# Token-major projections in 512-column matmuls over two k-halves, and rotations placed first in their panel

## What is computed

```python
# first block, layer 0 (even mixer): 512 + 256 tokens
px = hx @ w_in_even; pc = hc @ w_in_even          # each (tokens, 8 * 512)
qa, ka, va, ga, bb, cb, ub, gb = split(px, 8)      # qa, ka are rotated (axial_rope); va is the V of attention
out_b = short_conv(bb, cb, ub, conv_w) * silu(gb)
# first block, layer 1 (odd mixer)
qn, kn, vn, gn, ud, gd = split(hx @ w_in_odd, 6)   # vn is the V of neighbourhood attention
# second block, layer 1: chunked spatial gating
z = gelu(h @ sgu_w_in)                             # (512, 2 * 3072)
u, v = split(z, 2)
v = layer_norm(v, ln_g, ln_b)                      # over 3072 features of a token
sv = einsum("gts,bcsgd->bctgd", tril(w_s), v_chunks) + b_s
out = (u * sv) @ w_out
```

## Time and profile before

| | |
|---|---|
| median of 3 runs | 2531.35 us (2530.65 to 2531.72) |
| the profiled execution | 2530.41 us, of which the span of instructions is 2528.7 us |
| TensorE matmul (PE) | 2335.9 us busy, 92% |
| VectorE (DVE) | 1411.4 us busy, 56% |
| ScalarE (ACT) | 589.1 us busy, 23% |
| GpSimd (POOL) | 88.3 us busy, 3% |
| mean granted TensorE clock | 0.935 of full speed |
| DMA | 196.03 MB, mean 78 GB/s |

### The profile page before, as it was taken

The page is one execution under the profiler, slowest core; times in us unless marked ns, Lnnn a source line. Parts: engine busy times, 40 slices in busy tenths (PEclk is TensorE's granted clock), DMA queues, the critical chain, the costliest instruction groups (busy, mean ns, idle before and its releaser), DMA issues.

```text
span 2528.7 us, 28943 instructions
## 1 busy us (share of the span) xinstructions
PE 2335.9 (92%) x12276; PEld 1911.6 (76%) x12276; DVE 1411.4 (56%) x1673; ACT 589.1 (23%) x1138; POOL 88.3 (3%) x57
## 2 busy tenths in 40 slices
PE   6999898999899978886799999999999999999997
PEld 5787786678879744675478888889988787888886
DVE  2332346774561177565857776354388735777633
ACT  2111015661320256125621111011110001111100
POOL 0000000000000122022100000000000000000000
PEclk9899998669799989997899999999999999999998
DMA  8022130001122101120012222322222122222222
GB/s 337 18 100 100 67 117 34 18 1 51 34 84 67 68 24 57 62 72 1 34 67 85 99 100 79 103 85 84 101 82 83 65 91 97 84 100 100 79 92 79
DMA packets 30704, 196.03 MB, mean 78 GB/s; under 512 B 3440, under 2 KB 3696, under 8 KB 12528
## 3 DMA queue, kind: packets, MB, share of 16 engines
q1 hardware_dynamic: 29136, 188.03, 21.1%
q10 hardware_dynamic: 1440, 6.16, 0.7%
HBM read 192.08 MB, written 2.10 MB: 77 GB/s over the span
## 4 chain that ended last, share of the span: by engine, by line
PE 84%; DVE 11%; ACT 2%; issue 1%; POOL 1%; DMA 1%; SPq 0%; DVEq 0%; ACTq 0%; POOLq 0%
PE ps L329 20%; PE ps L330 20%; PE ps L331 20%; PE ps L385 3%; PE ps L386 3%; PE ps L387 3%; PE ps L482 2%; PE ps L556 2%; PE ps L438 2%; PE ps L767 1%; PE ps L744 1%; PE ps L587 1%; PE ps L422 1%; PE ps L920 1%; PE ps L463 1%
## 5 line engine op out<-in xcount | busy, mean ns | idle before, releaser
L1414 DVE CAST whi<-raw 128x2048 fp32r<-128x2048 f32 (+2 forms) x162 | 183.8, 1135 | 482.2 <-DMA raw<-in_ffn_out 117.4
L329 PE MATMUL ps<-h2hi,whi 128*128 128x512 f32 x1040 | 409.4, 394 | 18.3 <-DVE h2lo L1511 12.1
L330 PE MATMUL ps<-h2lo,whi 128*128 128x512 f32 x1040 | 407.0, 391 | 0.0
L331 PE MATMUL ps<-h2hi,wlo 128*128 128x512 f32 x1040 | 406.7, 391 | 0.0
L1415 DVE TENSOR_TENSOR wlo<-raw,whi 128x2048 fp32r<-128x2048 f32 (+2 forms) x162 | 341.5, 2108 | 5.6
L329 PE MATMUL ps<-h1hi,whi 128*128 128x512 f32 (+1 forms) x768 | 278.0, 362 | 16.1 <-DVE h1lo L1456 8.0
L330 PE MATMUL ps<-h1lo,whi 128*128 128x512 f32 (+1 forms) x768 | 272.7, 355 | 0.0
L331 PE MATMUL ps<-h1hi,wlo 128*128 128x512 f32 (+1 forms) x768 | 270.6, 352 | 0.0
L329 PEld LDWEIGHTS ps<-h2hi,whi 128*128 128x128 f32 x1040 | 196.7, 189 | 61.2 <-issue 13.8
L331 PEld LDWEIGHTS ps<-h2hi,wlo 128*128 128x128 f32 x1040 | 196.7, 189 | 40.9
L330 PEld LDWEIGHTS ps<-h2lo,whi 128*128 128x128 f32 x1040 | 196.9, 189 | 40.5
(11 more groups left out here) (247 smaller groups left out, 3583.4 us busy)
## 6 DMA issues: line engine op xcount, KB each, us to landing
raw<-in_ffn_in SPq DMA_DIRECT2D x44, 1024.0 KB, 4.8
raw<-in_ffn_out SPq DMA_DIRECT2D x32, 704.0 KB, 4.1
raw<-in_even SPq DMA_DIRECT2D x16, 1024.0 KB, 6.9
mod_w<-in_mod SPq DMA_DIRECT2D x6, 2048.0 KB, 25.6
mraw<-in_mod SPq DMA_DIRECT2D x12, 1024.0 KB, 4.9
raw<-in_odd SPq DMA_DIRECT2D x12, 1024.0 KB, 4.9
raw<-in_sgu_v SPq DMA_DIRECT2D x12, 1024.0 KB, 4.8
raw<-in_sgu_u SPq DMA_DIRECT2D x12, 1024.0 KB, 4.8
```

The lines of the kernel that those rows point to most:

```text
L329: pe.matmul(o, r(lhi), r(rhi), start=first, stop=False, **kw)
L330: pe.matmul(o, r(lhi), r(rlo), start=False, stop=False, **kw)
L331: return pe.matmul(o, r(llo), r(rhi), start=False, stop=last, **kw)
L1414: step(dve.tensor_copy(whi[:, slot, 0:width].bitcast(F32R), raw[:, slot, 0:width]))
```

## The change

The three token-major projections are stored in DRAM in another order (`_wide_panels`): a pair of panels now holds 512 output features, the first panel the blocks kt 0 to 3 of them and the second the blocks 4 to 7. Each panel has the size that it had. A token tile's matmuls are 512 columns wide, fill a bank of their own, and accumulate over both panels; the banks of a pair stay taken from its first panel to the end of its second. In the second panel each tile is finished by itself and told by a new semaphore `wide_done` (the last by `panel_done`), and ScalarE evicts tile by tile, 512 columns at a time.

In the even projections the banks are handed over in other steps: panel 4 begins after `e_free` 3, panel 6 after `e_free` 5 (which ScalarE now tells after the third tile of the pair), and panels 7, 8 and 9 wait for `e_free` 6, 7 and 8. In the spatial gating the first pair fills banks 0 to 3 and the second banks 4 to 7: panel 2's first two tiles run before the spread, the third after it, and the fourth after the copy of the spread (`rx_copied`), since it takes bank 7.

VectorE's `rope(3)` stands ahead of the loop over j, and inside it `rope(4 + 2j)` and `rope(5 + 2j)` take the places of `rope(3 + 2j)` and `rope(4 + 2j)`, for j < 2: each of the rotations 4 to 7 stands one place earlier than it did.

```diff
...
+        EV_BANK, OV_BANK = (0, 1, 4, 2, 3, 5), (0, 1, 2, 3, 4, 5)
...
-            def paced_token_pair(n, hi, lo, parts_made):
-
-                pe.wait_ge(split_done, n + 2)
-                for kt in range(KT):
-                    pe.wait_ge(parts_made, kt + 1)
-                    for i in range(2):
-                        for t in range(4):
-                            last = token_part(n + i, 2 * i, t, kt, hi, lo, kt == 0 and t % 2 == 0,
-                                              kt == KT - 1, skip_group_check=True)
-                        if kt == KT - 1:
-                            last.then_inc(panel_done, 1)
+            def wide_part(n, bank, t, kt, hi, lo):
+
+                o = ps[:, bank, :]
+                lhi, llo = r(hi[:, kt, t * P:(t + 1) * P]), r(lo[:, kt, t * P:(t + 1) * P])
+                rhi, rlo = r(w(n, 0, kt % 4, width=512, cols=512)), r(w(n, 1, kt % 4, width=512, cols=512))
+                pe.matmul(o, lhi, rhi, start=kt == 0, stop=False)
+                pe.matmul(o, lhi, rlo, start=False, stop=False)
+                return pe.matmul(o, llo, rhi, start=False, stop=kt == KT - 1)
+
+            def wide_tile(n, half, bank, t, hi, lo):
+
+                for kt in range(4 * half, 4 * half + 4):
+                    last = wide_part(n, bank, t, kt, hi, lo)
+                return last
+
+            def wide_second_half(n, banks, hi, lo):
+
+                pe.wait_ge(split_done, n + 1)
+                for t, bank in enumerate(banks):
+                    last = wide_tile(n, 1, bank, t, hi, lo)
+                    if t < len(banks) - 1:
+                        last.then_inc(wide_done, 1)
+                last.then_inc(panel_done, 1)
...
-                if e in (4, 6, 8):
-                    pe.wait_ge(e_free, e)
+                if e in (6, 7, 8, 9):
+                    pe.wait_ge(e_free, e - 1)
                 elif e >= 10:
                     pe.wait_ge((zed, b_free)[s], (e - 8) // 2)
                 elif e in (2, 3):
                     pe.wait_ge(e_free, e - 1)
-                if e in (4, 5):
-                    token_panel(e, 3 * s, 6, h1hi, h1lo)
+                if e == 4:
+                    pe.wait_ge(split_done, e + 1)
+                    for t in range(6):
+                        if t in (0, 3):
+                            pe.wait_ge(e_free, 3 + t // 3)
+                        last = wide_tile(e, 0, EV_BANK[t], t, h1hi, h1lo)
+                    last.then_inc(panel_done, 1)
+                elif e == 5:
+                    wide_second_half(e, EV_BANK, h1hi, h1lo)
                 elif e == 0:
...
-            pe.wait_ge(o_free, 7)
-            token_panel(p0 + 8, 0, 6, h1hi, h1lo)
-            pe.wait_ge(o_free, 8)
-            token_panel(p0 + 9, 3, 6, h1hi, h1lo)
+            pe.wait_ge(split_done, p0 + 9)
+            for t in range(6):
+                if t in (0, 3):
+                    pe.wait_ge(o_free, 7 + t // 3)
+                last = wide_tile(p0 + 8, 0, OV_BANK[t], t, h1hi, h1lo)
+            last.then_inc(panel_done, 1)
+            wide_second_half(p0 + 9, OV_BANK, h1hi, h1lo)
...
-            paced_token_pair(p0, h2hi, h2lo, n_ok["mixpre1"])
+            for kt in range(KT):
+                if kt % 4 == 0:
+                    pe.wait_ge(split_done, p0 + kt // 4 + 1)
+                pe.wait_ge(n_ok["mixpre1"], kt + 1)
+                for t in range(4):
+                    last = wide_part(p0 + kt // 4, t, t, kt, h2hi, h2lo)
+                if kt % 4 == 3:
+                    last.then_inc(panel_done, 1)
             sums_added("mixpre1")
-            token_panel(p0 + 2, 4, 4, h2hi, h2lo)
+            pe.wait_ge(split_done, p0 + 3)
+            for t in range(2):
+                wide_tile(p0 + 2, 0, 4 + t, t, h2hi, h2lo)
             spread("mixpre1", range(4))
-            for n in range(3, 12):
-                pe.wait_ge(sg["v"], 4 * (n - 2))
-                token_panel(p0 + n, 2 * (n % 3), 4, h2hi, h2lo)
+            wide_tile(p0 + 2, 0, 6, 2, h2hi, h2lo)
+            pe.wait_ge(rx_copied, 3)
+            wide_tile(p0 + 2, 0, 7, 3, h2hi, h2lo).then_inc(panel_done, 1)
+            wide_second_half(p0 + 3, range(4, 8), h2hi, h2lo)
+            for g in range(2, 6):
+                base = 4 * (g % 2)
+                pe.wait_ge(split_done, p0 + 2 * g + 1)
+                for t in range(4):
+                    pe.wait_ge(sg["v"], 4 * (g - 2) + t + 1)
+                    last = wide_tile(p0 + 2 * g, 0, base + t, t, h2hi, h2lo)
+                last.then_inc(panel_done, 1)
+                wide_second_half(p0 + 2 * g + 1, range(base, base + 4), h2hi, h2lo)

             pe.wait_ge(sg["ws"], 1)
-            pe.wait_ge(sg["v"], 44)
+            pe.wait_ge(sg["v"], 20)
...
-                    pe.wait_ge(rx_copied, 3)
-                    pe.wait_ge(sg["v"], 48)
+                    pe.wait_ge(sg["v"], 24)
...
-                if e // 2 == 2:
-                    act.wait_ge(panel_done, e + 1)
-                    last = copy(ev[:, :, s * 256:(s + 1) * 256].rearrange("p (b t) n -> p b t n", t=2),
-                                ps[:, 3 * s:3 * s + 3, :].rearrange("p b (t n) -> p b t n", t=2))
+                if e == 4:
+                    continue
+                if e == 5:
+                    for t in range(6):
+                        if t < 5:
+                            act.wait_ge(wide_done, t + 1)
+                        else:
+                            act.wait_ge(panel_done, e + 1)
+                        last = copy(ev[:, t, :], ps[:, EV_BANK[t], :])
+                        if t == 2:
+                            tell(last, e_free, 5)
+                        elif t < 5:
+                            step(last)
...
+                if b < 4 or b == 5:
+                    act.wait_ge(panel_done, FIRST["odd"] + k + 1)
                 if b == 4:
-                    at = (0, 3)[s]
-                    last = copy(ov[:, :, s * 256:(s + 1) * 256].rearrange("p (b t) n -> p b t n", t=2),
-                                ps[:, at:at + 3, :].rearrange("p b (t n) -> p b t n", t=2))
+                    for t in range(3 * s, 3 * s + 3):
+                        if t < 5:
+                            act.wait_ge(wide_done, 6 + t)
+                        else:
+                            act.wait_ge(panel_done, FIRST["odd"] + 10)
+                        last = copy(ov[:, t, :], ps[:, OV_BANK[t], :])
+                        if t % 3 < 2:
+                            step(last)
...
-            for n in range(12):
-                b = 2 * (n % 3)
-                act.wait_ge(panel_done, FIRST["sgu_v"] + n + 1)
+            for g in range(6):
                 for t in range(4):
-                    copy(vtok[:, 2 * n:2 * n + 2, t, :],
-                         ps[:, b + t // 2, t % 2 * 256:t % 2 * 256 + 256].rearrange("p (d n) -> p d n", d=2),
+                    if g and t < 3:
+                        act.wait_ge(wide_done, 10 + 3 * (g - 1) + t + 1)
+                    else:
+                        act.wait_ge(panel_done, FIRST["sgu_v"] + 2 * g + 2)
+                    copy(vtok[:, 4 * g:4 * g + 4, t, :],
+                         ps[:, 4 * (g % 2) + t, :].rearrange("p (d n) -> p d n", d=4),
...
+            rope(3)
             for j in range(4):
-                if j < 3:
-                    rope(3 + 2 * j)
+                if j < 2:
+                    rope(4 + 2 * j)
                 split_at(9 + 2 * j)
                 dve.wait_ge(cb_in, j + 1)
                 step(dve.tensor_tensor(zpad[:, 514:770], eob[:, j, TX:TA], ps[:, 4, TC:2 * TC], ALU.mult))
                 tell(dve.tensor_tensor(zpad[:, 1:513], eob[:, j, 0:TX], ps[:, 1, :], ALU.mult), zed, j + 1)
                 if j < 2:
-                    rope(4 + 2 * j)
+                    rope(5 + 2 * j)
...
             def v_stats(i):
-                dve.wait_ge(sg["v"], 8 * (i + 1))
+                dve.wait_ge(sg["v"], 4 * (i + 1))
...
+def _wide_panels(w):
+
+    k, n = w.shape
+    return w.reshape(2, k // 2 // P, P, n // 512, 512).transpose(3, 0, 2, 1, 4).reshape(n // 256, P, -1)
...
```

More of the change, by code:

```diff
@@ L205, in build_kernel @@
         mod_rows, mod_cols = sem("mod_rows"), sem("mod_cols")
+        wide_done = sem("wide_tile_done")
         cond_ready = sem("cond_ready")
@@ L1166, in odd_out @@
                 b, s = k // 2, k % 2
-                act.wait_ge(panel_done, FIRST["odd"] + k + 1)
+                if b < 4 or b == 5:
+                    act.wait_ge(panel_done, FIRST["odd"] + k + 1)
                 if b == 4:
-                    at = (0, 3)[s]
-                    last = copy(ov[:, :, s * 256:(s + 1) * 256].rearrange("p (b t) n -> p b t n", t=2),
-                                ps[:, at:at + 3, :].rearrange("p b (t n) -> p b t n", t=2))
+                    for t in range(3 * s, 3 * s + 3):
[6 more added lines that the diff above has]
+                            step(last)
                 else:
@@ L2082 @@
```

(9 more changed lines are left out.)

## The result

The changed kernel took 2489.05 us (median of 4 runs, 2485.23 to 2492.51) against 2531.0 us (median of 4, 2529.27 to 2531.72) for the kernel before on the same chip: a ratio of 0.9837, 95% interval 0.9824 to 0.9849. Faster, as forecast, but by 42.0 us instead of 33.3. The forecast of 2498.0 us is 8.95 us too high, and the time lies 0.95 us under the low end of the range. The profiled execution of the changed kernel took 2490.41 us, its span is 2488.7 us, 40.0 less than the 2528.7 of before.

The account below looks back on a forecast made before the run. TensorE, busy 92% of the span, was taken as the bound, to be relieved by a shorter stream or closed gaps. Terms of 16.44, 3.11, 1.91, 11.34 and 0.5 us summed to 33.3, giving 2498.0 us, range 2490 to 2507.

Parts of the forecast that it names:

- (a): VectorE's rotations 4 to 7, moved earlier: TensorE's waits ahead of panels 9 to 11 go, 16.44 us won.
- (b): Even token-major pair: wide matmuls win 1.92 us and panel 6's shorter wait 1.19 us, sum 3.11 us.
- (c): Odd token-major pair: 144 matmuls of 512 columns take 32.64 us instead of 34.55, 1.91 us won.
- (d): Spatial gating, v: 576 matmuls replace 1152, 7.66 us, and panel 3's wait goes, 3.68 us; 11.34 us in all.
- (e): End of v: one eviction left after the last matmul instead of four; between 0 and 1.0 us, taken as 0.5.
- The rival by which a wait stays or takes another place: Rotation waits of TensorE: one remaining costs about 5.5 us, all three 16.4; 2503.5 to 2514.4 us, chance 0.08.
- The rival of dear wide matmuls: Wide projections: moving weight columns cost up to 0.2400 us per matmul, 11.5 us less gain, 2509.5 us; chance 0.06.
- The rival of the falling clock: Wide tiles: bank handovers lower the clock, 0.427 us per wide matmul; slower, 2584 us with half of them; chance 0.03.
- One reading against it: Spatial gating's first pair: it already changed banks every three matmuls and had granted clock 1.00.
- This one did not cost any clock before: Wait of panel 3 in the spatial gating: 3.68 us won, with no further gain from the clock.
- the doubt behind the 0.5: End of v: VectorE's earlier work might last until 1.93 us after TensorE's end if the load lands as late.
- the step on the clock elsewhere: Stages behind the changed ones, including attention: nothing found that shifts them, a few us possible, 2490 to 2506; chance 0.07.

Follow-up runs that it names:

- run 2: The changed kernel with VectorE's rotations back in their old places, leaving the wide projections alone; 2511.11 us, ratio 0.9922.
- run 9: The kernel before with four more 512-column matmuls ahead of panel 12, well before the attention stage; 2530.14 us, ratio 1.0.
- run 10: The kernel before with eight more 512-column matmuls ahead of panel 12, well before the attention stage; 2528.07 us, ratio 1.0003.
- run 5: The kernel before with only VectorE's rotations 4 to 7 one place earlier, measured and profiled a second time; 2506.26 us, ratio 0.9917.
- run 1: The kernel before with only VectorE's rotations 4 to 7 one place earlier, first measurement; 2506.47 us (median of 10), ratio 0.9926.
- run 3: The changed kernel measured and profiled again, code unchanged; 2491.69 us, ratio 0.9843.
- run 6: The changed kernel with four more 512-column matmuls ahead of panel 12, well before the attention stage; 2493.55 us, ratio 0.9855.
- run 8: The changed kernel with twelve more 512-column matmuls ahead of panel 12, well before the attention stage; 2492.17 us, ratio 0.9846.

## Why the prediction missed

**The sum was right.** By its own steps, profile against profile:

| part | forecast | measured |
|---|---|---|
| (a) rotations 4 to 7 | 16.44 | 16.47 (93.24 to 76.77) |
| (b) even pair, and its wait | 3.11 | 3.15 (38.13 to 34.98, from the first rotation to panel 6) |
| (c) odd pair | 1.91 | 1.89 (34.55 to 32.66) |
| (d) `sgu_v` to line 900, now 942 | 11.34 | 11.26 (146.28 to 135.02) |
| (e) end of `sgu_v` | 0.5 | 0.88 (15.24 to 14.36) |
| sum | 33.3 | 33.65 |

The left number of each pair is from the profile that the forecast was read from, so the agreement tests the changed side alone. That side holds: over the seven profiles with the wide code the even pair takes 34.98 us, the odd pair 32.65 to 32.66, `sgu_v` 134.95 to 135.22 and its end 14.36. The other side varies. With the rotations in their old places, the way from the rotation ahead of panel 8 to that ahead of panel 11 took 72.66 us here, 73.04 in run 2 and 71.78 and 71.21 in runs 9 and 10 (57.58 wherever they were moved), and `sgu_v` of before took 146.3 us in two profiles and 148.6 in three (runs 5, 9 and 10). So (b) and (c) are firm, while it is luck that (a) came within 0.03 us and (d) within 0.08: against another profile of before (a) would have been off by up to 1.5 us and (d) by 2.3.

(a) The idle time was 11.02 us, and 5.4 us more came back because the clock no longer falls in the gaps, as priced. The cost of the move was nothing, as said, for the reason given: VectorE's timeline of the changed kernel has the split of panel 9 behind the rotation, waiting for its load and not for the rotation:

```profile
222.87 0.69 DVE L1629 TENSOR_TENSOR eq<-eq,temp 128x512 f32<-128x512 f32 x1
...
227.62 1.23 DVE L1472 CAST whi<-raw 128x2048 fp32r<-128x2048 f32 x1 [4.06 <-DMA raw<-in_even]
```

The rotation ends 4.06 us before the load has landed. The rival by which a wait stays or takes another place has nothing for it.

(b), (c), (d) The rival of dear wide matmuls fell: 0.2266 us with the weights moving, as with the activations moving. The Trainium skill (TensorE: Matmul & The Clock Gate, "Wait — 56ns, not 53.3ns?") gives a fixed cost of about 2.5 ns per matmul; an estimate by that figure makes the odd pair 0.36 us shorter. The trace disagrees: 1.89 us for 144 matmuls that went, 13.1 ns each. The rival of the falling clock fell too, with 1.00 granted in the windows of the wide tiles. One reading against it was wrong: before, the first pair of `sgu_v` changed banks every six matmuls, since two tiles shared a bank, and not every three. The changed kernel does change every three there, and its TensorE was busy for 24.20 us of the 24.20 from 1666.8 to 1691.0.

(d) "This one did not cost any clock before", said of the wait of panel 3, is true of the profile of before and of run 1 alone. In runs 5, 9 and 10, with the same code, the clock fell in that wait and stayed down for 6.8 us, which made `sgu_v` 2.3 us longer. No profile with the wide code has that spell. So in three of five executions this part of the change was worth 13.6 us and not 11.3.

(e) The term was 0.38 us too small, inside its bounds. ScalarE evicts the last tile in 0.69 us and VectorE's statistics follow 0.98 us after TensorE's end (the first row of ScalarE's timeline, the second of VectorE's):

```profile
1802.00 0.69 ACT L985 ACTIVATE vtok<-ps,root 128x512 f32<-128x512 f32 x1 [2.03 <-PE ps L406]
```

```profile
1802.78 2.88 DVE L1938 BATCH_NORM_STATS2 bns<-vtok 128x6 f32<-128x512 f32 x4 [0.33 <-ACT vtok L985]
```

VectorE idles 0.33 us there, so work left over from earlier tiles does not hold it, which was the doubt behind the 0.5.

**What failed** is the step on the clock elsewhere: "I find nothing that shifts them, but a few us either way are possible, 2490 to 2506", with a chance of 0.07. The sum has no term for it, so the stages that the diff does not touch were put at no change. Measured, they gave 6.3 us beyond the sum, 5.7 of them in the attention stage. The trace of before showed, and I did not weigh, that its largest single uncertainty was not in the changed code. The third quarter of the attention stage ran at 0.50 with TensorE busy for 51.77 of 52.60 us; the stage takes 166.7 to 191.0 us over profiles of kernels that are the same in it, and two executions of one kernel differ by over 20 us.

Profile against profile, the span fell by 40.0 us, 6.3 beyond the sum: 5.7 in this stage, 1.0 in `sgu_u` (278.74 to 277.71 us, with 3.4 us on the lower clock instead of 6.8), 0.9 at the end (19.20 to 18.28, 13.0 instead of 17.0), 1.2 ahead of the first rotation, and 2.5 given back in other stages. Against the medians, 42.0 us: 33.6 are the sum and about 3.6 more lie in the rest (37.2 - 33.6), of which some 1.6 is the spell in `sgu_v`, in two of the three profiles of before. The last 4.8 are left for an attention stage that is typically shorter. That is an inference: the profiles give 169.9 us on average for the five of the changed kernel and 177.5 for the three of before, each with a spread wider than the difference.

That the time fell outside the range is partly luck. All eight runs of the changed kernel together have a median of 2490.4 us, the second four alone 2491.69, inside the range; 0.95 us is less than the 2.6 by which two sets of four runs of this kernel differ. All 47 runs of the kernel before have 2530.7, so the gain is nearer 40.3 us than 42.0. The error of the mechanism is there all the same, 7 us of 40.

**What stays open** is why, and how firmly, the changed kernel gets the shorter stage more often. The wide code is not needed for it (run 5 has it with the rotations alone, run 9 with neither) and does not ensure it (run 2). The medians seem to point to the rotations: alone they gained 25.0 and 24.4 us for a part worth 16.5, the wide code alone 20.3 for parts worth 17.2. But by the mean of their 14 runs the rotations gained 19.5 us, 3.0 beyond their part, because some executions take the long stage. What changes is how often each course of the clock comes up, and four to twelve runs of a kernel do not measure that. So the range was set too narrow at the low end: with the stage anywhere between 166.7 and 191.0 us in place of 174.7, the 2498.0 us of the sum become 2490.0 to 2514.3, and with the 3.6 us of the spells elsewhere they begin at 2486.4.

No run points to a version that beats the changed kernel; the medians of runs 3, 6 and 8, 2491.69 to 2493.55 us, are the same within the spread.

## What to carry to other kernels

Price each matmul start to start in an undisturbed stream of its own shape, and each wait together with the clock that it costs: here five terms worked out in this way came within 0.4 us each, and the executions of before themselves differ by 2 us in two of these places. A hand-ordered engine queue gains most where the step that another engine asks for stands directly behind what it needs, ahead of a product that waits for the next panel. And before giving a range, look through the stages that the change does not touch for stretches on the lower clock: one that TensorE bounds at mixed clocks can move the time by more than the change's own uncertainty, so take several profiles and compare many runs, their spread and mean as well as their median. A wait that cost no clock in one profile may cost it in the next.

## What was not expected of the hardware

- A matmul of 512 columns cost 0.2266 us whether weights or activations moved, and 13 ns less than two of 256.
- TensorE stayed on its lower clock for 52.6 us in which it was busy 98% of the time (51.77 us), and one 512-column matmul more per unit did not change that time (98.5 against 100.7 us).
- One kernel, started twice, took 166.8 and 191.0 us for one stage with the same instructions, and three different kernels took the same 166.7 to 166.8 us with 95.2 to 95.3 us on the lower clock. Whether the clock fell 3.60 or 3.69 us before the stage's first reciprocal went with 190.9 or 166.8 us.
- 0.34 us of length for each us on the lower clock is less than the half that a stage bound by TensorE throughout would show; VectorE is busy for 138 to 140 us of the stage, at every clock.
- The same idle time ahead of panel 3, 3.63 us, made the clock fall in three of five executions and not in the other two.
- Twelve runs of the code of before with eight matmuls more reach from 2515.61 to 2549.46 us, while their median stays within 0.1% of it.
